# Memory keys by row pieces over four banks, token transposes inside the value projection, first convolution tap on ScalarE

## The chip, the core and the metric

One core of one Trainium2 chip runs the whole layer. The metric is device time in microseconds (us) of one execution. Engines: TensorE (PE in the profile, its weight loads PEld), VectorE (DVE), ScalarE (ACT), GpSimd (POOL) and SyncE (SP), which issues all transfers.

## What is computed

A decoder layer on 256 tokens of width 1024: LayerNorm, a token mixer with three branches (gated delta rule, short convolution, attention into 256 memory tokens), LayerNorm, 32 routed experts of which each token uses four, LayerNorm. The change touches what stands at the start of the mixer:

```python
h = layer_norm(x, ln0_g, ln0_b)
proj = x @ w_in                       # qkv, a, bt, z, xc, gb, gc, qm, gl
qkv = silu(causal_depthwise_conv(qkv, conv_qkv))      # width 4
g = -(exp(a_log) * softplus(a + dt_bias)); beta = sigmoid(bt)
kv = mem @ w_mem_kv; km, vm = split(kv, 2)
```

## The kernel before

All projections of the mixer are made in three products, high part times high part, high times low, low times high, so that single-precision passes suffice. A weight column block of 512 (a "slot", 2 MB) is loaded into one of three raw buffers. It is used in four pieces of 1024 columns per partition. For each piece ScalarE casts the high part (`w_hi`, L1048), and VectorE or GpSimd subtracts it for the low part (`w_lo`, L759); `LO_ENGINE` says which of the two. There are three pairs of piece buffers, so the cast of piece q+3 waits until TensorE has finished with piece q.

One list, `SCHEDULE`, made by `mixer_schedule`, sets the order on every engine: TensorE, ScalarE, VectorE and GpSimd each walk through it and do their part of each entry, so an entry that waits holds back all that follows it on its engine. A "unit" is an entry with a PSUM bank; units take banks 0 to 2 in turn, and one can't start until the bank of the unit three before it is free. Banks 3 to 7 serve the delta rule later.

The start goes like this. SyncE loads the first key columns, the memory tokens (1 MB), three more key column pieces (each 128 columns, rows of 512 bytes), the value columns (2 MB), the tokens `hx` (1 MB), LayerNorm's two parameter rows, small rows, and then the qkv slots. TensorE warms up with ten products (L1222), turns the memory tokens (`memT`, four units, L1244), makes the keys (`km`, four units, one head each, each over all eight row blocks: L1171 to L1173), then the values (`vm`, two units, 128x512 outputs, four row pieces), then turns the normalised tokens (`hT`, four units, L1258), then makes the twelve qkv units of 24 products each (a group of eight "triples"). Between the second and the third stand the eight decay columns (`ab`), then their turn (`abT`).

VectorE does LayerNorm in `ln`: statistics (L1506, L1509), reciprocal, two passes over a tile (L1521, L1523), with ScalarE's root (L1020) in between. Each qkv unit gets four taps on VectorE, a product with a column scalar (L1632) and three multiply-adds (L1635), and the silu on ScalarE (L1027). The decay columns are split on VectorE (`ab split`, L1565, L1566), and their softplus is built from VectorE's min and max (L1655 to L1657) and ScalarE's functions (L1068 to L1071). GpSimd makes all masks at the start (L944 to L965), the per-level ones behind its eighth piece.

After the mixer each expert takes six chunks of 2 MB through a ring of twelve (`chunk_dma`, L792). The second expert's chunks wait until the mixer's last output product is there.

## Time and profile before

| | |
|---|---|
| median of 3 runs | 1269.95 us (1269.81 to 1270.58) |
| profiled execution | 1270.24 us, span 1268.5 us |
| mean granted TensorE clock | 0.987 |
| PE busy | 1218.5 us, 96% |
| DVE, ACT, POOL busy | 400.8, 239.2, 141.1 us (32%, 19%, 11%) |
| DMA | 453.45 MB, 357 GB/s over the span |
| chain that ended last | PE 78%, DMA 9%, SPq 4%, DVE 4% |

The mixer fills the first 340 us or so, the experts the rest. A row of the timeline gives start, duration, engine, line, operation and, in brackets, the idle time before it and what ended that; a group of the lines view gives busy time and mean duration; a window gives the busy time of each engine, the granted clock (PEclk, 1.00 is 2.4 GHz and 0.50 is 1.2 GHz) and the transfers. Matmuls are pipelined, so printed durations overlap, and the spacing of starts tells the pace.

### The profile page before, as it was taken

How to read it: one execution, taken by the hardware profiler on the slowest of the kernel's cores; microseconds unless marked ns; L12 is line 12 of the kernel's file. 1: busy time of each engine (PE TensorE's matmuls, PEld its weight loads, DVE VectorE, ACT ScalarE, POOL GpSimd, SP SyncE). 2: the span in 40 equal slices, each digit the busy share in tenths (PEclk: the TensorE clock that was granted, in tenths of full speed). 3: DMA queues.
4: the chain of work that ended last, by engine and by line, in shares of the span. 5: the costliest groups of instructions: out<-in, count | busy, mean ns of one | idle time of the engine just before them, and what ended most of it. 6: DMA issues, size and time to landing. Idle time of an engine off the chain costs nothing.

```text
span 1268.5 us, 17229 instructions
## 1 busy us (share of the span) xinstructions
PE 1218.5 (96%) x7155; PEld 616.8 (49%) x7155; DVE 400.8 (32%) x787; ACT 239.2 (19%) x385; POOL 141.1 (11%) x105
## 2 busy tenths in 40 slices
PE   8799999999999999999999999999999999999995
PEld 7699999998843333333333333333333333333332
DVE  5685563534521221222222122122122222222114
ACT  4364344444310000010000000000000000000001
POOL 4433422455200000000000000000000000000000
PEclk9899999999999999999999999999999999999998
DMA  9533313595799999999999999999999999999995
GB/s 306 198 134 134 134 68 134 205 360 184 281 399 424 428 427 428 427 428 428 430 428 430 428 427 428 430 428 430 428 427 427 429 427 429 429 426 428 428 427 209
DMA packets 56412, 453.45 MB, mean 357 GB/s; under 512 B 6877, under 2 KB 11050, under 8 KB 31786
## 3 DMA queue, kind: packets, MB, share of 16 engines
q1 hardware_dynamic: 56362, 452.71, 86.3%
q8 instruction: 40, 0.66, 0.2%
q14 instruction: 10, 0.08, 0.0%
HBM read 451.64 MB, written 1.05 MB: 357 GB/s over the span
## 4 chain that ended last, share of the span: by engine, by line
PE 78%; DMA 9%; SPq 4%; DVE 4%; ACT 2%; issue 2%; POOL 0%; another core or an unknown queue 0%; DVEq 0%; ACTq 0%
PE bank L1357 30%; PE bank L1429 15%; DMA late<-in_w_gate_up_dram 8%; PE bank L1171 5%; PE bank L1172 5%; PE bank L1173 5%; PE bank L1328 4%; PE bank L1442 4%; SPq L792 4%; PE bank L1343 2%; PE bank L1417 2%; ACT late L1143 1%; DMA early<-in_ln_b_dram 1%; PE bank L1437 1%; DVE w_lo L759 1%
## 5 line engine op out<-in xcount | busy, mean ns | idle before, releaser
L1357 PE MATMUL bank<-late 128*64 128x512 f32 x1536 | 343.2, 595 | 5.1 <-DMA late<-in_w_gate_up_dram 5.1
L1429 PE MATMUL bank<-late 128*64 128x512 f32 x1024 | 230.1, 602 | 6.2 <-ACT late L1143 6.2
L1357 PEld LDWEIGHTS bank<-late 128*64 128x64 f32 x1536 | 106.7, 137 | 222.7 <-issue 209.8
L1429 PEld LDWEIGHTS bank<-late 128*64 128x64 f32 x1024 | 71.4, 138 | 142.9 <-issue 129.1
L1171 PE MATMUL bank<-act_hi,w_hi 128*128 128x256 f32 x448 | 129.4, 289 | 3.1 <-DVE early L1635 2.5
L1172 PE MATMUL bank<-act_lo,w_hi 128*128 128x256 f32 x448 | 125.8, 281 | 0.0
L1173 PE MATMUL bank<-act_hi,w_lo 128*128 128x256 f32 x448 | 125.8, 281 | 0.0
L1775 DVE TENSOR_SCALAR late<-bank 128x512 f32<-128x512 f32 x32 | 22.1, 692 | 308.2 <-PE bank L1357 308.2
L1357 PE MATMUL bank<-raw,late 128*64 128x512 f32 x512 | 116.7, 598 | 1.2 <-DMA raw<-in_w_gate_up_dram 1.2
L759 POOL TENSOR_TENSOR w_lo<-raw,w_hi 128x1024 fp32r<-128x1024 f32 x33 | 81.2, 2463 | 127.1 <-ACT w_hi L1048 127.1
L1171 PEld LDWEIGHTS bank<-act_hi,w_hi 128*128 128x128 f32 x448 | 84.3, 188 | 5.3 <-DVE early L1635 3.3
L1172 PEld LDWEIGHTS bank<-act_lo,w_hi 128*128 128x128 f32 x448 | 84.5, 189 | 0.1
L1173 PEld LDWEIGHTS bank<-act_hi,w_lo 128*128 128x128 f32 x448 | 84.4, 188 | 0.0
L1786 DVE COPY late<-bank 64x512 f32<-64x512 f32 x32 | 22.2, 694 | 191.3 <-PE bank L1429 191.3
L1136 ACT COPY late<-bank 128x512 f32<-128x512 f32 x33 | 19.3, 586 | 321.9 <-PE bank L1328 321.9
L1048 ACT CAST w_hi<-raw 128x1024 fp32r<-128x1024 f32 x56 | 58.5, 1046 | 90.2 <-issue 59.4
L1357 PEld LDWEIGHTS bank<-raw,late 128*64 128x64 f32 x512 | 34.0, 136 | 72.3 <-issue 69.0
L1442 PE MATMUL bank<-late 64*128 64x512 f32 x256 | 63.6, 615 | 1.0 <-DVE late L1846 1.0
L1145 ACT COPY late<-bank 64x512 f32<-64x512 f32 x32 | 18.5, 579 | 233.3 <-PE bank L1429 233.3
L1328 PE MATMUL bank<-hx,late 128*64 128x512 f32 x264 | 62.3, 592 | 0.0
L1141 ACT ACTIVATE late<-late 128x512 f32<-128x512 f32 x32 | 20.1, 629 | 179.7 <-DVE late L1775 179.7
L1790 DVE COPY late<-bank 128x256 f32<-128x256 f32 x31 | 13.2, 425 | 117.9 <-PE bank L1437 117.9
(319 smaller groups left out, 1194.4 us busy)
## 6 DMA issues: line engine op xcount, KB each, us to landing
late<-in_w_gate_up_dram SPq DMA_DIRECT2D x96, 2048.0 KB, 36.4
late<-in_w_down_dram SPq DMA_DIRECT2D x64, 2048.0 KB, 35.8
raw<-in_w_gate_up_dram SPq DMA_DIRECT2D x32, 2048.0 KB, 34.5
raw<-in_w_in_dram SPq DMA_DIRECT2D x8, 2048.0 KB, 8.7
...
```

What stands on the lines that cost most here:

```text
L759: ops.tensor_tensor(lo, src, as_f32(hi), ALU.subtract).then_inc(split_lo[who], 1)
L792: sp.dma_start(dst, src).then_inc(landed, 16)
L1048: a.copy(hi, src).then_inc(split_hi, 1)
L1171: mm(o, l_hi, r_hi, start=start, stop=False)
L1172: mm(o, l_hi, r_lo, start=False, stop=False)
L1173: return mm(o, l_lo, r_hi, start=False, stop=stop)
L1328: ins = mm(ps[0][64 * c:64 * c + 64, :], onehot[:, t, :], hx[:, t, 512 * c:512 * (c + 1)], start=(t == 0), stop=(t == NT - 1))
L1343: mm(ps[1 + n][64 * c:64 * c + 64, :], e_row[rows, :], bgu[rows, :], start=True, stop=False)
L1357: ins = mm(bk[64 * c:64 * c + 64, :], x_slotT[:, k % 4, 64 * (k // 4):64 * (k // 4) + 64], w[:, kk, at + 512 * c:at + 512 * (c + 1)], star ...
L1417: ins = tr(ps[3][:, c * P:(c + 1) * P], h_tok[:, c:4 * P:4], ident[:])
L1429: ins = mm(ps[3][64 * c:64 * c + 64, :], hidT[:, kk, 64 * q:64 * q + 64], w[:, kk, c * 512:(c + 1) * 512], start=(q == 0 and kk == 0), sto ...
L1442: ins = mm(ps[4 + 2 * t + c][:, :], scatter[64 * c:64 * c + 64, t * P:(t + 1) * P], y_tok[64 * c:64 * c + 64, :], start=False, stop=True, ...
```

## The change

- **Loads.** The memory tokens come first, then key pieces 0 and 1, the tokens, key pieces 2 and 3, LayerNorm's rows, then the value columns in four pieces. All eight key and value pieces are row pieces (256 rows of 512 columns, rows of 2 KB), each with a semaphore. The router's weights move behind slot 5.
- **Keys.** The four heads are made together in banks 4 to 7: for each row piece, 2 row blocks for each of four heads; ScalarE copies all four at the end. Statistics and roots of both tiles come ahead of the keys, the passes in between.
- **Tokens.** The transposes go to banks 4 to 7 too and stand inside the value projection, tile 0 behind its second row piece, tile 1 behind the first tile's third.
- **Who subtracts.** Pieces 0 to 11: DVE, POOL, DVE, POOL, three DVE, two POOL, DVE, POOL, DVE.
- **ScalarE** takes the first tap of each qkv unit (a copy with a column scale), the cast of the decay columns, and the signs and relu of the softplus.
- **GpSimd** makes four of seven block masks first, three behind piece 1, the decay masks behind piece 3, the level masks one by one behind pieces 10 to 20, the chunk masks behind 22.

```diff
@@ -103,10 +103,12 @@
 
 
 
-    order = [("prep", 0)] + [("memT", n) for n in range(4)] + [("prep", 1), ("prep", 2)]
-    order += [("km", n) for n in range(4)] + [("ln", 0, t) for t in range(NT)] + [("vm", n) for n in range(NT)]
-    order += [("hT", t, j) for j in range(2) for t in range(NT)] + [("prep", 9), ("cols",), ("prep", 10)]
-    order += [("qkv", 0), ("ab split",), ("qkv", 1), ("ab", 0), ("qkv", 2), ("abT", 0), ("qkv", 3), ("decay functions",)]
+    order = [("memT", 0), ("prep", 0), ("memT", 1), ("prep", 1), ("memT", 2), ("memT", 3)]
+    order += [("ln stats", t) for t in range(NT)] + [("prep", 2), ("prep", 3)] + [("ln root", t) for t in range(NT)]
+    order += [("km", 0), ("ln", 0, 0), ("prep", 4), ("prep", 5), ("ln", 0, 1), ("prep", 6), ("km copy",), ("prep", 7), ("prep", 8)]
+    order += [("hT", t, j) for t in range(NT) for j in range(2)] + [("prep", 9), ("vm", 0), ("prep", 10), ("vm", 1), ("cols",)]
+    order += [("ab split",)]
+    order += [("qkv", 0), ("qkv", 1), ("ab", 0), ("qkv", 2), ("abT", 0), ("qkv", 3), ("decay functions",)]
...
@@ -392,6 +398,10 @@
 
 
         piece_end, joint = {}, 0
+        for q in PIECES_OF["km", 0]:
+            joint += 1
+            piece_end[q] = (joint_piece, joint) if joint < 4 else (km_full, H)
+        joint = 3
...
@@ -404,7 +414,7 @@
 
 
         LO_ENGINE = ["pool" if q % 2 == 0 or MIXER_SLOTS[q // 4][0] == "br" else "dve" for q in range(4 * N_MIX)]
-        LO_ENGINE[0:12] = ["dve"] * 5 + ["pool"] * 4 + ["dve"] * 3
...
@@ -770,10 +781,14 @@
                 src = m.rearrange("(k p) n -> p k n", p=P)[:, :, c:c + W]
             if n >= RAW:
                 raw_spent(sp, n - RAW)
-            if n == 0:
-                sp.dma_start(dst[:, :, j * P:(j + 1) * P], src[:, :, j * P:(j + 1) * P]).then_inc(piece_in[j], 16)
+            if kind == "kv":
+                sp.dma_start(dst[:, 2 * j:2 * j + 2, :], src[:, 2 * j:2 * j + 2, :]).then_inc(piece_in[4 * n + j], 16)
             else:
                 sp.dma_start(dst, src).then_inc(raw_in[n % RAW], 16)
+
...
@@ -827,14 +842,16 @@
             def bcast(dst, src, done):
                 sp.dma_start(dst, src).then_inc(done, 16)
 
+            sp.dma_start(mem_tok, mem[0].rearrange("(t p) d -> p t d", p=P)).then_inc(mem_in, 16)
             slot_dma(sp, 0, 0)
-            sp.dma_start(mem_tok, mem[0].rearrange("(t p) d -> p t d", p=P)).then_inc(mem_in, 16)
-            for j in range(1, 4):
-                slot_dma(sp, 0, j)
-            slot_dma(sp, 1)
+            slot_dma(sp, 0, 1)
             sp.dma_start(hx[:], x[0].rearrange("(t p) d -> p t d", p=P)).then_inc(x_in, 16)
+            slot_dma(sp, 0, 2)
+            slot_dma(sp, 0, 3)
             bcast(lnp0[:, 0, :], ln0_g.rearrange("(a d) -> a d", a=1).broadcast_to([P, D]), lnp_in[0])
             bcast(lnp0[:, 1, :], ln0_b.rearrange("(a d) -> a d", a=1).broadcast_to([P, D]), lnp_in[0])
+            for j in range(4):
+                slot_dma(sp, 1, j)
...
@@ -1030,16 +1051,16 @@
             a.activation(ln_std[:, 0:1], eps_ln, ACT.Sqrt)
             for s in SCHEDULE:
                 kind = s[0]
-                if kind in ("memT", "hT", "km", "vm", "z", "xc", "gb", "qm", "gate", "pT", "ym", "x1T"):
+                if kind in ("memT", "vm", "z", "xc", "gb", "qm", "gate", "pT", "ym", "x1T"):
                     act.wait_ge(bank_full[bank_of(s)], turn_of(s))
                 free = bank_free[bank_of(s)] if kind not in NOT_UNITS else None
                 if kind == "prep":
                     q = s[1]
                     n = q // 4
-                    if n == 0:
+                    if n < 2:
                         act.wait_ge(piece_in[q], 16)
                     else:
-                        act.wait_ge(raw_in[n % RAW], 16 * len(range(n % RAW or RAW, n + 1, RAW)))
+                        act.wait_ge(raw_in[n % RAW], 16 * len(range(first_fill(n % RAW), n + 1, RAW)))
                     if q >= SPLITS:
                         act.wait_ge(*piece_end[q - SPLITS])
...
@@ -1050,25 +1071,42 @@
                     a.copy(src_hi[:, 2 * s[1]:2 * s[1] + 2, :], bank(s, 512).rearrange("p (a b) -> p a b", a=2)).then_inc(bank_hi, 1)
                 elif kind == "hT":
                     t, j = s[1:]
+                    act.wait_ge(h_turned, 2 * t + j + 1)
                     a.copy(act_hi[:, 4 * j:4 * j + 4, t * P:(t + 1) * P],
-                           bank(s, 512).rearrange("p (a b) -> p a b", b=P)).then_inc(bank_hi, 1)
-                elif kind == "ln":
+                           ps[4 + 2 * t + j][:, :].rearrange("p (a b) -> p a b", b=P)).then_inc(bank_hi, 1)
+                elif kind == "ln root":
+                    ln_root_of(0, s[1])
+                elif kind == "ln" and s[1] == 1:
                     ln_root_of(*s[1:])
-                elif kind == "km":
-                    a.copy(kmT[:, s[1], :], bank(s)).then_inc(free, 1)
+                elif kind == "km copy":
+                    for n in range(H):
+                        act.wait_ge(km_full, n + 1)
+                        a.copy(kmT[:, n, :], ps[4 + n][:, 0:T]).then_inc(km_copied, 1)
+                elif kind == "ab split":
+                    act.wait_ge(ab_in, 16)
+                    a.copy(w_ab_hi[:], w_ab).then_inc(ab_hi, 1)
                 elif kind == "vm":
                     a.copy(vm[:, s[1], :], bank(s, 512)).then_inc(free, 1)
                 elif kind == "qkv":
+                    if s[1] == 0:
+                        act.wait_ge(cols_ready, 1)
+                    act.wait_ge(bank_full[bank_of(s)], turn_of(s))
+                    a.activation(qkvT[:, s[1], :], bank(s), ACT.Copy,
+                                 scale=small_cols[:, 36 + s[1]:37 + s[1]]).then_inc(first_tap, 1)
                     if s[1] >= 1:
                         silu(s[1] - 1)
                     if s[1] == 11:
                         silu(11)
                 elif kind == "decay functions":
-                    act.wait_ge(ab_dve, 1)
-                    a.activation(ea, adt[:, 0, :], ACT.Exp)
-                    a.activation(beta, beta, ACT.Exp, scale=-1.0)
-                    step(a.activation(t_b, t_b, ACT.Exp))
-                    a.activation(t_b, t_b, ACT.Ln, bias=1.0).then_inc(ab_act, 2)
+                    act.wait_ge(bank_free[bank_of(("abT", 0))], turn_of(("abT", 0)))
+                    a.activation(t_c, pre_g, ACT.Relu)
+                    step(a.activation(t_b, pre_g, ACT.Abs))
+                    step(a.activation(ea, adt[:, 0, :], ACT.Exp))
+                    a.mul(ea, ea, -1.0)
+                    step(a.activation(beta, beta, ACT.Exp, scale=-1.0))
+                    a.activation(beta, beta, ACT.Identity, bias=1.0)
+                    step(a.activation(t_b, t_b, ACT.Exp, scale=-1.0))
+                    a.activation(t_b, t_b, ACT.Ln, bias=1.0).then_inc(ab_act, 1)
                 elif kind == "z":
...
@@ -1176,13 +1214,35 @@
 
                 hi, lo = piece(PIECES_OF[s][-1])
                 for k in range(nk):
-                    if s == ("km", 0) and k % 2 == 0:
-                        wait_copied(pe, "memT", k // 2 + 1)
                     if s == ("qkv", 0) and k % 4 == 0:
-                        wait_copied(pe, "hT", 2 + k // 2)
+                        pe.wait_ge(h_split, 3 + k // 4)
                     ins = three(ps[bank_of(s)][:, 0:T], hi[:, k, c * P:(c + 1) * P], lo[:, k, c * P:(c + 1) * P],
                                 rhs_hi[:, k, :], rhs_lo[:, k, :], k == 0, k == nk - 1)
                 ins.then_inc(bank_full[bank_of(s)], 1)
+
+            def project_keys():
+
+                for j in range(4):
+                    hi, lo = piece(PIECES_OF["km", 0][j])
+                    wait_copied(pe, "memT", j + 1)
+                    for n in range(H):
+                        for kk in range(2):
+                            k = 2 * j + kk
+                            ins = three(ps[4 + n][:, 0:T], hi[:, kk, n * P:(n + 1) * P], lo[:, kk, n * P:(n + 1) * P],
+                                        src_hi[:, k, :], src_lo[:, k, :], k == 0, k == KD - 1)
+                        if j == 3:
+                            ins.then_inc(km_full, 1)
+                    if j < 3:
+                        ins.then_inc(joint_piece, 1)
+
+            def turn_tile(t):
+
+                pe.wait_ge(ln_done, t + 1)
+                pe.wait_ge(km_copied, H)
+                for j in range(2):
+                    for k in range(4):
+                        ins = tr(ps[4 + 2 * t + j][:, k * P:(k + 1) * P], hx[:, t, (4 * j + k) * P:(4 * j + k + 1) * P], ident[:])
+                    ins.then_inc(h_turned, 1)
 
             def project_rows(s, lhs_hi, lhs_lo, sums=False, apart=False):
...
@@ -1194,6 +1254,8 @@
                 if apart:
                     order = order[:4] + [(j, t) for t in range(NT) for j in (2, 3)]
                 for j, t in order:
+                    if s == ("vm", 0) and j == 2:
+                        turn_tile(t)
                     u = both[t]
                     hi, lo = piece(PIECES_OF[s][j])
...
@@ -1547,23 +1609,25 @@
                 if kind == "prep":
                     prep_lo(v, d, s[1], "dve")
                     continue
+                if kind == "ln stats":
+                    t = s[1]
+                    if t == 0:
+                        v.wait_ge(x_in, 16)
+                    step(half_stats(t, 0))
+                    step(half_stats(t, 1))
+                    variance(t)
+                    continue
                 if kind == "ln":
                     n, t = s[1:]
                     if n == 0:
-                        if t == 0:
-                            v.wait_ge(x_in, 16)
-                        step(half_stats(t, 0))
-                        step(half_stats(t, 1))
-                        variance(t)
                         v.wait_ge(lnp_in[0], 32)
                         normalise(0, t, lnp0)
                     else:
                         normalise(1, t)
                     continue
                 if kind == "ab split":
```

How it moves the instructions, at three places. ScalarE at the start (`raw` to `w_hi` is a piece's cast, `bank` to `src_hi` a memory block, `bank` to `early` a key head's copy). Before:

```order
L1048 CAST w_hi<-raw 128x1024 [waits piece_in0]
L1050 CAST src_hi<-bank0 128x512 [waits bank_full0]
L1050 CAST src_hi<-bank1 128x512 [waits bank_full1]
L1050 CAST src_hi<-bank2 128x512 [waits bank_full2]
L1050 CAST src_hi<-bank0 128x512 [waits bank_full0]
L1048 CAST w_hi<-raw 128x1024 [waits piece_in1]
L1048 CAST w_hi<-raw 128x1024 [waits piece_in2]
L1048 CAST w_hi<-raw 128x1024 [waits split_lo_dve,bank_full1,piece_in3]
L1058 COPY early<-bank1 128x256 [waits bank_full1]
L1048 CAST w_hi<-raw 128x1024 [waits split_lo_dve,bank_full2,raw_in1]
L1058 COPY early<-bank2 128x256 [waits bank_full2]
```

In the change:

```order
L1071 CAST src_hi<-bank0 128x512 [waits bank_full0]
L1069 CAST w_hi<-raw 128x1024 [waits piece_in0]
L1071 CAST src_hi<-bank1 128x512 [waits bank_full1]
L1069 CAST w_hi<-raw 128x1024 [waits piece_in1]
L1071 CAST src_hi<-bank2 128x512 [waits bank_full2]
L1071 CAST src_hi<-bank0 128x512 [waits bank_full0]
L1069 CAST w_hi<-raw 128x1024 [waits piece_in2]
L1069 CAST w_hi<-raw 128x1024 [waits split_lo_dve,joint_piece,piece_in3]
L1041 ACTIVATE tiny<-tiny 128x1 [waits ln_var] x2
L1069 CAST w_hi<-raw 128x1024 [waits split_lo_pool,joint_piece,piece_in4]
```

The casts of pieces 0 and 1 stand between the memory blocks, and the wait for a bank of a key unit has become one for a piece (`joint_piece`).

TensorE where the tokens are turned (`hx`; L1258 before, L1244 now). Before, at the end of the values:

```order
L1173 MATMUL bank0<-w_hi,src_lo 128x512
L1258 MATMUL bank1<-ident,hx 128x128 [waits ln_done,bank_free1]
L1258 MATMUL bank1<-ident,hx 128x128 x3
L1258 MATMUL bank2<-ident,hx 128x128 [waits ln_done,bank_free2]
L1258 MATMUL bank2<-ident,hx 128x128 x3
L1258 MATMUL bank0<-ident,hx 128x128 [waits ln_done,bank_free0]
L1258 MATMUL bank0<-ident,hx 128x128 x3
```

In the change, inside them:

```order
L1211 MATMUL bank2<-w_hi,src_lo 128x512
L1244 MATMUL bank4<-ident,hx 128x128 [waits km_copied,ln_done]
L1244 MATMUL bank4<-ident,hx 128x128 x3
L1244 MATMUL bank5<-ident,hx 128x128 x4
L1209 MATMUL bank1<-w_hi,src_hi 128x512 [waits split_lo_dve]
```

The transposes wait for the key copies and the tile, no longer for the units' banks, and value products follow them at once.

VectorE between the memory blocks and LayerNorm's passes. Before:

```order
L1626 TENSOR_TENSOR src_lo<-bank0,src_hi 128x512 [waits bank_hi]
L759 TENSOR_TENSOR w_lo<-raw,w_hi 128x1024 [waits split_hi] x4
L1506 BN_STATS tiny<-hx 128x6 [waits x_in]
L1506 BN_STATS tiny<-hx 128x6 [waits dve_chain]
L1509 BN_AGGR tiny<-tiny 128x2 [waits dve_chain]
L1516 RECIPROCAL tiny<-tiny 128x1 [waits ln_root,lnp0_in]
L1521 SCALAR_TENSOR_TENSOR hx<-hx,tiny,early 128x1024 [waits ln_var,dve_chain]
L1523 SCALAR_TENSOR_TENSOR hx<-hx,tiny,early 128x1024 [waits dve_chain]
```

In the change:

```order
L1691 TENSOR_TENSOR src_lo<-bank0,src_hi 128x512 [waits bank_hi]
L1568 BN_STATS tiny<-hx 128x6 [waits x_in]
L1568 BN_STATS tiny<-hx 128x6 [waits dve_chain]
L1571 BN_AGGR tiny<-tiny 128x2 [waits dve_chain]
L1568 BN_STATS tiny<-hx 128x6
L1568 BN_STATS tiny<-hx 128x6 [waits dve_chain]
L1571 BN_AGGR tiny<-tiny 128x2 [waits dve_chain]
L770 TENSOR_TENSOR w_lo<-raw,w_hi 128x1024 [waits split_hi]
L1578 RECIPROCAL tiny<-tiny 128x1 [waits ln_root,lnp0_in]
L1583 SCALAR_TENSOR_TENSOR hx<-hx,tiny,early 128x1024 [waits ln_var,dve_chain]
```

The low part of the third piece (the one L770 row) stands behind both tiles' statistics.

## Rows read from the trace of the kernel before

**Rows 1.** Page, part 2: GB/s of all DMA in each of the 40 slices
```profile
GB/s 306 198 134 134 134 68 134 205 360 184 281 399 424 428 427 428 427 428 428 430 428 430 428 427 428 430 428 430 428 427 427 429 427 429 429 426 428 428 427 209
```

**Rows 2.** Chain that ended last, 1040 to 1268.5: start us, us, what
```profile
1181.68 48.84 DMA late<-in_w_gate_up_dram
```

**Rows 3.** Windows of 5 us: PE, PEld, DVE, ACT, POOL busy, PEclk, DMA, GB/s
```profile
330.00:335.00 5.00, 5.00 (x23) 4.01 (x22) 1.79 (x3) 0.38 (x1) 2.34 (x7) 1.00 0.72 262
```

**Rows 4.** Timeline, SyncE, 334 to 345: start us, us, queue line op
```profile
336.37 1.28 SPq L792 DMA_DIRECT2D late<-in_w_gate_up_dram  x3
```

**Rows 5.** Timeline, TensorE: start us, us, operation [idle before, what ended it]
```profile
7.44 3.42 PE L1244 MATMUL bank<-ident,early 128*128 128x128 f32 x16 [2.14 <-DMA early<-in_mem_dram]
...
34.48 0.50 PE L1171 MATMUL bank<-w_hi,src_hi 128*128 128x512 f32 x1 [3.48 <-POOL w_lo L759]
...
51.91 0.28 PE L1171 MATMUL bank<-act_hi,w_ab_hi 128*8 128x256 f32 x1 [4.14 <-DVE w_ab_lo L1566]
...
63.63 0.38 PE L1171 MATMUL bank<-act_hi,w_hi 128*128 128x256 f32 x1 [1.13 <-DVE early L1635]
...
95.26 0.39 PE L1171 MATMUL bank<-act_hi,w_hi 128*128 128x256 f32 x1 [1.41 <-DVE early L1635]
```

**Rows 6.** Windows of 2 us, TensorE alone: busy, PEclk, DMA share, GB/s
```profile
8.00:10.00 2.00, 2.00 (x11) 0.50 1.20 291
...
52.00:54.00 2.00, 2.00 (x11) 0.53 1.05 396
...
62.00:64.00 2.00, 0.87 (x8) 1.00 0.00 0
```

**Rows 7.** Groups by line, TensorE, 12:22, 23:30, 35:39, 336:342: xcount, busy us, mean ns
```profile
L1173 PE MATMUL bank<-src_hi,w_lo 128*128 128x256 f32 x29 | 8.2, 281 | 0.0
...
L1171 PE MATMUL bank<-w_hi,src_hi 128*128 128x512 f32 x10 | 4.0, 395 | 0.0
...
L1173 PE MATMUL bank<-w_hi,src_lo 128*128 128x512 f32 x4 | 2.3, 569 | 0.0
...
L1258 PE MATMUL bank<-ident,hx 128*128 128x128 f32 x16 | 2.1, 274 | 0.4 <-DVE hx L1519 0.4
```

**Rows 8.** Windows of 2 us, all engines, value columns in rows of 2 KB
```profile
14.00:16.00 2.00, 2.00 (x18) 2.00 (x18) 1.74 (x2) 1.32 (x2) 0.00 (x0) 1.00 1.06 390
```

**Rows 9.** Timeline, ScalarE: casts, a bank copy, a table load, short function, silu
```profile
11.38 2.00 ACT L1048 CAST w_hi<-raw 128x1024 fp32r<-128x1024 f32 x2
...
14.96 0.36 ACT L1058 COPY early<-bank 128x256 f32<-128x256 f32 x1
...
64.05 1.28 ACT L1068 ACT_TABLE_LOAD   x1
...
66.47 0.19 ACT L1069 ACTIVATE tiny<-tiny 128x8 f32<-128x8 f32 x1
...
70.59 0.42 ACT L1027 ACTIVATE early<-early 128x256 f32<-128x256 f32 x1
```

**Rows 10.** Timeline, VectorE: low parts, statistics, tile passes, decay cast, taps
```profile
12.46 2.36 DVE L759 TENSOR_TENSOR w_lo<-raw,w_hi 128x1024 fp32r<-128x1024 f32 x2 [0.26 <-ACT w_hi L1048]
...
21.95 1.42 DVE L1506 BATCH_NORM_STATS2 tiny<-hx 128x6 f32<-128x512 f32 x2 [1.43 <-DMA hx<-in_x_dram]
...
24.86 2.43 DVE L1521 SCALAR_TENSOR_TENSOR hx<-hx,tiny,early 128x1024 f32<-128x1024 f32 x1
...
27.33 1.28 DVE L1523 SCALAR_TENSOR_TENSOR hx<-hx,tiny,early 128x1024 f32<-128x1024 f32 x1
...
49.28 2.15 DVE L1565 CAST w_ab_hi<-early 128x64 fp32r<-128x64 f32 x1
...
61.55 0.48 DVE L1632 TENSOR_SCALAR early<-bank,small_cols 128x256 f32<-128x256 f32 x1
...
62.06 1.52 DVE L1635 SCALAR_TENSOR_TENSOR early<-bank,small_cols,early 128x255 f32<-128x255 f32 x3
```

**Rows 11.** Timeline, GpSimd: low part beside VectorE's pass
```profile
23.81 2.40 POOL L759 TENSOR_TENSOR w_lo<-raw,w_hi 128x1024 fp32r<-128x1024 f32 x1 [0.38 <-ACT w_hi L1048]
```

114 lines of the change are left out of this document (60 added, 54 removed).

## The prediction

> **What bounds the kernel now.** Read the page by slices first, then the chain that ended last, the DMA windows, and only then the start. The 40 slices (31.7 us each) show 424 to 430 GB/s from the thirteenth to the last but one, and a stream with gaps before [rows 1]. The chain agrees at its end: the last link before the last expert's products is a weight chunk, 48.84 us from issue to landing [rows 2], so the expert stage ends when its weights have come. The windows tell since when the stream is unbroken: the engines still idle a quarter of the time at 330 to 335 us [rows 3]. SyncE issues three chunks of the second expert from 336.37 [rows 4], when the last output product of the mixer is there. What follows is a fixed amount of bytes at a fixed rate, about 932 us to the end of the span (1268.5). The expert stage, 73% of the span, is thus a rigid block behind the mixer's last product, and TensorE's work in it hangs on the same point. A microsecond taken out of TensorE's path in the mixer is one off the total; a faster expert stage isn't in this change.
>
> In the mixer TensorE is the path, and its holes stand at the start: 2.14 us before the memory tokens are turned, 3.48 before the last value product, 4.14 before the decay columns, 1.13 before the fifth qkv unit, then 1.41 at 95 us [rows 5]. Three of them also cost clock: the granted clock is 0.50 behind the first (1.2 of 2.4 GHz) and 0.53 behind the third; it stays at 1.00 around the hole of 1.13 [rows 6]. Behind the second hole a 128x512 product takes 569 ns, against 395 at full clock [rows 7].
>
> **The ledger.** I count TensorE's time up to the fifth qkv unit, which starts at 63.63 now [rows 5]. All its products stay; only order and waits change. At full clock 29 triples fit in 10 us at width 256 (0.35 each), 10 in 7 us at width 512 (0.70), and 16 transposes take 2.1 us [rows 7].
>
> *Landing.* The memory tokens go first. Now they land at 7.44 behind a half-megabyte column piece; without it, 0.52 MB at between 291 and 390 GB/s, 1.3 to 1.8 us earlier: 5.9. Row pieces then come in 2 KB rows. The window with column pieces (512 B rows) gave 291 GB/s, one with whole rows 390 [rows 8]. At 390 a piece (0.52 MB) takes 1.3 us and the tokens (1.05 MB) 2.7: piece 0 at 7.2, piece 1 at 8.6, tokens at 11.3, pieces 2 and 3 at 12.7 and 14.0, LayerNorm's rows near 17, value pieces from 18. At 291 all of it would be later by a third, 3 us at piece 3; this end is kept for the range.
>
> *Keys.* ScalarE's cast is 1.0 us in a row of casts [rows 9], VectorE's subtraction 1.2, GpSimd's 2.4 [rows 10, 11]. Piece 0: cast 7.3 to 8.3, low part to 9.6, so the keys start at 9.6 (10.55 now). 32 triples are 11.2 us. Piece 1 goes to GpSimd and is ready at 12.4, as the first 2.8 us end. Piece 2 goes to VectorE but stands behind both tiles' statistics. Two halves take 1.42 and the aggregate 0.2; four memory subtractions end at about 12.0, so the statistics end at 15.2, and the low part at 16.4, where the products of piece 1 end at 15.3: a wait of **1.0**.
>
> *Values and token transposes.* 16 triples of 0.70 are 11.2; the 16 transposes inside them 2.1 at full clock. Their inputs: low parts of value pieces 0 and 1 at 22, normalised tiles at 20.6 and 25.9 (two passes of 1.28 [rows 10] behind LayerNorm's rows and the interleaved low parts), key copies at 24.9, all before TensorE wants them (22, 25, 28, 31 us). The 3.48 hole goes: piece 3 of the values is cast behind the first value piece, not behind the second tile's root. If that cover were gone, up to 3.5 us would come back.
>
> *Decay columns.* The 4.14 hole consists of three taps, the cast of the columns (2.15 [rows 10], the span in which GpSimd runs a subtraction) and their subtraction, all on VectorE behind the first unit. Now ScalarE casts (0.2) and VectorE subtracts ahead of the first taps, under 11 us of products. The hole and its slow clock go. Small turn 0.2, five groups of 8 triples 14.0, turn of the decay rows 0.2.
>
> *First tap.* VectorE loses 12 operations of 0.48 [rows 10], ScalarE gains 12. The trace has no scaled copy of 128x256 from a bank: below it the plain copy, 0.36, above it the silu, 0.42 [rows 9]; I take 0.42, since it reads a scale. It runs beside the low part, so of the bank's return, cast 1.05, low part 1.25, three taps 1.52 [rows 10], it adds nothing on odd pieces and the bank comes back 0.5 earlier. The hole of 1.13 behind the short decay unit becomes 0.9.
>
> *Decay signs.* ScalarE now does eight short functions (0.2 each, chained; four before) and two table loads of 1.28 in one go [rows 9], about 4.1 us. This holds back the cast for the eighth unit: about 0.45 us of wait. The hole of 1.41 shrinks by 0.5. These two cancel.
>
> *Masks.* Four levels end by 7.7 and three run between subtractions; per-level masks, 0.8 us each, fill GpSimd behind even pieces, in a stretch where it has one 2.4 us subtraction per two units (5.7 us). They cost nothing unless VectorE's subtraction meets one (0.5). Router weights move four loads later and are needed 290 us later: nothing. SyncE reaches all it is moved past earlier than now.
>
> *Hand-offs and clock at the start.* 0.8 for some ten new waits near the edge, 0.5 for slow clock around 8 us (0 if the warm-up carries over, 1.8 if it is as behind the 3.48 hole [rows 5, 7]: some 12 products at 0.38 instead of 0.23 apart).
>
> Sum: 9.6 + 11.2 + 1.0 + 11.2 + 2.1 + 0.2 + 14.0 + 0.2 + 0.9 + 0.8 + 0.5 = 51.7, or 52.2 with the rounding of triples (0.354). 63.63 − 52.2 = **11.4 us**. The profiled execution took 1270.24 (span 1268.5); that less 11.4 is **1258.8**. The median shown is 0.3 lower, which is noise here.
>
> **Where it is tight.** The low part of piece 2 (VectorE, ready to start at 15.2) and of piece 3 (GpSimd, ready at 14.0 + 1.05 = 15.1 to 15.6) reach their engines within half a microsecond. The trace shows what a meeting costs: the pass over a tile that starts at 24.86 takes 2.43, its twin 1.28 [rows 10], while GpSimd's 2.40 from 23.81 runs [rows 11]: it did nothing until GpSimd was done. [...]
>
> **Rivals.**
> 1. *GpSimd gets in first.* Piece 2's low part ends at 18.7, the wait is 3.3 instead of 1.0, and a hole of 3.48 was followed by the half clock (1.8 us). Plus 4.1: **1262.9**. For it: tokens landed late in this trace (21.95 [rows 10], though issued at 8.96). Against it: pieces land late too, which holds GpSimd back.
> 2. *Better than the ledger.* Rows land at full rate, neither the 1.0, the 0.8 nor the 0.5 shows and the taps' hole closes: 3.2 less, **1255.6**.
> 3. *The gain is hidden.* If the stream were bound by something of its own, nothing would move: **1270.2**. Against it: the windows before 335 us, in which DMA idles [rows 3], and the issue that waits for the mixer [rows 4].
> 4. *Slower: a split before each piece.* The keys now stop at each quarter. If each split starts only when the piece before it is being used and the two engines lock each other out, a hole of 3.3 and a slow restart of 1.8 stand before each of four pieces: 4 x 5.1 − 1.0 = 19.4 more, **1278**. It decides from the third such piece on (14.3 > 11.4). For it: one product group per piece is 2.8 us, less than cast plus GpSimd's 2.4. Against it: three buffers, and pieces alternate engines. The Trainium skill, TensorE: Matmul & The Clock Gate, section HAM oscillation — how this bites in real kernels, describes this pattern, a wait behind each short group that drops the clock again each time; this trace shows such drops behind the holes of 2.14, 3.48 and 4.14 and none at 1.13 [rows 5 to 7]; no run here shows them in a row.
>
> **How the numbers follow.** Forecast 0.47, rival one 0.33, two 0.13, three 0.03, four 0.04. The range runs from just above rival two, 1255.8, to above rival one with a little of slow landing, 1264. A difference of 0.2% (2.5 us) is what can be told from no change. Faster needs under 1267.4: forecast and the first two rivals, 0.93. Same 0.03, slower 0.04.
>
> **What would show it.** Right: memory transposes start near 6 and keys at 9.5; one hole of about 1 us before the third key piece and none over 1 before 50; the decay columns start without a hole; the fifth qkv unit starts at 52, the unbroken stream near 325; clock 1.00 from 12 us on. A subtraction of 2 us or more at 15 with 0.50 clock behind it is rival one. Four holes of 3 us with a clock drop behind each are rival four. Wrong altogether: a mixer that ends 11 us earlier and a span that doesn't.

## The result, and the profile after

| | before | change |
|---|---|---|
| median of the runs made side by side | 1269.88 us (1269.34 to 1270.58, 4) | 1255.13 us (1254.24 to 1257.27, 4) |
| profiled execution, its span | 1270.24, 1268.5 | 1255.70, 1254.0 |
| mean granted clock | 0.987 | 0.994 |
| PE, DVE, ACT, POOL busy | 1218.5, 400.8, 239.2, 141.1 | 1213.0, 390.5, 243.5, 148.7 |
| DMA | 357 GB/s over the span | 362 GB/s |

The ratio is 0.9887, interval 0.9875 to 0.9899: 14.75 us less by the medians. The forecast was 11.4 less, 1258.8, in a range from 1255.8. So the kernel is faster by the expected way, and by 3.4 us more than forecast, 0.7 us beyond the lower end of the range.

Page of the change, parts 2 and 4: bandwidth by slice, then the shares of the chain that ended last.

```profile
GB/s 335 221 148 143 70 136 67 330 292 201 353 409 429 428 429 428 427 429 429 429 428 429 429 429 428 429 428 430 428 429 427 427 427 428 429 427 428 428 427 198
...
PE 78%; DMA 8%; SPq 5%; DVE 3%; ACT 3%; issue 2%; POOL 0%; DVEq 0%; ACTq 0%
```

From the thirteenth slice to the last but one it reads as in [rows 1], 427 to 430 GB/s. The block of expert weights is as rigid as it was; it only begins earlier. Its chunks, in SyncE's part of the timeline (start, duration, line, operation, count), first of the kernel before, then of the change. The row of before is the whole group whose last three chunks [rows 4] show:

```profile
330.44 21.24 SPq L792 DMA_DIRECT2D late<-in_w_gate_up_dram  x5
```

```profile
315.57 21.13 SPq L807 DMA_DIRECT2D late<-in_w_gate_up_dram  x5
```

The group starts 14.9 us earlier. The windows of 5 us around it in the change (columns as in [rows 3]):

```profile
315.00:320.00 5.00, 5.00 (x23) 4.01 (x22) 1.79 (x3) 0.52 (x1) 2.48 (x7) 1.00 0.72 261
320.00:325.00 5.00, 4.57 (x35) 3.99 (x34) 4.03 (x10) 1.81 (x6) 0.00 (x0) 1.00 0.86 321
325.00:330.00 5.00, 4.75 (x43) 4.54 (x43) 3.89 (x17) 2.28 (x6) 0.00 (x0) 1.00 1.01 433
```

The window at 315 (261 GB/s, 23 products) is the image of the one at 330 before [rows 3]: the same work 15 us earlier. The stream is unbroken from 325.

TensorE's timeline in the change (start, duration, line, operation; in brackets the idle time before and what ended it):

```profile
7.89 0.66 PE L1308 MATMUL bank<-ident,early 128*128 128x128 f32 x4 [0.53 <-DVE src_lo L1691]
9.63 0.38 PE L1209 MATMUL bank<-src_hi,w_hi 128*128 128x256 f32 x1 [1.09 <-DVE w_lo L770]
...
15.80 0.39 PE L1209 MATMUL bank<-src_hi,w_hi 128*128 128x256 f32 x1 [0.23 <-DVE w_lo L770]
...
21.71 0.50 PE L1209 MATMUL bank<-w_hi,src_hi 128*128 128x512 f32 x1
...
27.40 1.03 PE L1244 MATMUL bank<-ident,hx 128*128 128x128 f32 x8
...
34.76 0.36 PE L1209 MATMUL bank<-act_hi,w_hi 128*128 128x256 f32 x1
...
40.53 0.28 PE L1209 MATMUL bank<-act_hi,w_ab_hi 128*8 128x256 f32 x1
...
50.14 0.39 PE L1209 MATMUL bank<-act_hi,w_hi 128*128 128x256 f32 x1 [0.63 <-DVE early L1699]
...
81.55 0.39 PE L1209 MATMUL bank<-act_hi,w_hi 128*128 128x256 f32 x1 [0.81 <-DVE early L1699]
```

Against [rows 5]: the holes of 3.48 and 4.14 are gone (the tokens' transposes and the decay columns follow the product before them with none), and the one of 2.14 has become 0.53. The hole before the fifth qkv unit is 0.63 (1.13 before), and the one before the sixteenth unit 0.81 (1.41). The keys start at 9.63, the values at 21.71, the first qkv unit at 34.76, the fifth at 50.14 (63.63 before) and the sixteenth at 81.55 (95.26). The gain is thus 13.5 us at the fifth unit, 13.7 at the sixteenth, 14.5 at the end of the span.

The 13.5 are of two kinds. The holes printed up to the fifth unit add up to 11.5 us before and to 2.5 in the change. The half clock behind three of them, in windows from 7 to 12, 35 to 39 and 52 to 56 us, held back 5.1 us of products before (an estimate: one minus the granted clock, summed over windows of 1 us), and nothing in the change. By that estimate 5.1 of the 13.5 are clock and the rest is waiting. One window of 2 us from the middle stretch of before, TensorE alone:

```profile
36.00:38.00 2.00, 2.00 (x6) 0.50 1.04 395
```

VectorE, then GpSimd, at the third and fourth key piece:

```profile
11.47 1.42 DVE L1568 BATCH_NORM_STATS2 tiny<-hx 128x6 f32<-128x512 f32 x2
...
14.58 1.17 DVE L770 TENSOR_TENSOR w_lo<-raw,w_hi 128x1024 fp32r<-128x1024 f32 x1
...
16.80 2.28 DVE L1583 SCALAR_TENSOR_TENSOR hx<-hx,tiny,early 128x1024 f32<-128x1024 f32 x1
19.11 1.29 DVE L1585 SCALAR_TENSOR_TENSOR hx<-hx,tiny,early 128x1024 f32<-128x1024 f32 x1
```

```profile
9.90 2.42 POOL L770 TENSOR_TENSOR w_lo<-raw,w_hi 128x1024 fp32r<-128x1024 f32 x1 [2.19 <-ACT w_hi L1069]
...
15.09 2.90 POOL L770 TENSOR_TENSOR w_lo<-raw,w_hi 128x1024 fp32r<-128x1024 f32 x1 [0.60 <-ACT w_hi L1069]
```

The meeting that rival one was about did come, but the other way round. VectorE was in 0.5 us before GpSimd, kept its 1.17, and it was GpSimd that took 2.90 in place of 2.42. The later pass over a tile, which starts at 16.80 within GpSimd's 2.90, took 2.28; its twin at 19.11 took 1.29, as in [rows 10].

ScalarE's new work, the first tap and the decay signs with their two table loads:

```profile
50.54 0.47 ACT L1094 ACTIVATE early<-bank,small_cols 128x256 f32<-128x256 f32 x1
...
51.22 0.20 ACT L1102 ACTIVATE tiny<-tiny 128x8 f32<-128x8 f32 x1
...
51.53 1.28 ACT L1104 ACT_TABLE_LOAD   x1
...
53.73 1.28 ACT L1109 ACT_TABLE_LOAD   x1
55.02 0.21 ACT L1109 ACTIVATE tiny<-tiny 128x8 f32<-128x8 f32 x1
```

The tap takes 0.47 (0.42 was assumed), and the signs with all eight functions go from 51.22 to 55.23, 4.0 us (4.1 forecast).

### The profile page after: what moved, and what is told of

Read it like the earlier page. It is cut to its first block, busy times and chain, and to the rows that moved or that the text cites. A ratio compares the mean times of both kernels' runs of the same rounds, so it can differ in the third digit from the quotient of the medians.

```text
span 1254.0 us, 17233 instructions
## 1 busy us (share of the span) xinstructions
PE 1213.0 (97%) x7155; PEld 613.1 (49%) x7155; DVE 390.5 (31%) x768; ACT 243.5 (19%) x402; POOL 148.7 (12%) x106
## 4 chain that ended last, share of the span: by engine, by line
PE 78%; DMA 8%; SPq 5%; DVE 3%; ACT 3%; issue 2%; POOL 0%; DVEq 0%; ACTq 0%
PE bank L1419 29%; PE bank L1491 15%; DMA late<-in_w_gate_up_dram 8%; PE bank L1209 6%; SPq L807 5%; PE bank L1210 5%; PE bank L1211 5%; PE bank L1504 4%; PE bank L1390 4%; PE bank L1405 2%; PE bank L1479 1%; ACT late L1181 1%; ACT w_hi L1069 1%; PE bank L1499 1%; DMA raw<-in_w_mem_kv_dram 0%
## 5 line engine op out<-in xcount | busy, mean ns | idle before, releaser
L770 POOL TENSOR_TENSOR w_lo<-raw,w_hi 128x1024 fp32r<-128x1024 f32 x33 | 81.9, 2483 | 102.1 <-ACT w_hi L1069 102.0
## 6 DMA issues: line engine op xcount, KB each, us to landing
raw<-in_w_mem_kv_dram SPq DMA_DIRECT2D x8, 512.0 KB, 11.2
```

The lines of the kernel that those rows point to most:

```text
L770: ops.tensor_tensor(lo, src, as_f32(hi), ALU.subtract).then_inc(split_lo[who], 1)
```

## The experiments

In each the change is the base unless another is named. A median is of the number of runs in brackets. The mark used throughout is where the sixteenth unit starts, 81.55 in the first profile of the change and 81.82 in the second, so a difference of 0.3 there is nothing. "Later" is counted from 81.55.

**The memory second** (`mem_second`): the old order of the first two loads.

```diff
-            sp.dma_start(mem_tok, ...).then_inc(mem_in, 16)
             slot_dma(sp, 0, 0)
+            sp.dma_start(mem_tok, ...).then_inc(mem_in, 16)
```

> The change, but the first key piece is loaded ahead of the memory tokens, as before. Theory A (the gain is holes and slow clock ahead of the fifth qkv unit): the tokens land 1.3 us later, at 7.2 instead of 5.9, the memory transposes start behind a hole of 1.3 to 2 and partly at the slow clock, the keys start at 10.3 to 11 instead of 9.6, and the total rises by 0.7 to 2.5 us. Rival B (the load order of the first megabytes doesn't matter, because value pieces and LayerNorm's rows set the pace later): 0 within 0.3 us.

1257.64 us (4). The memory blocks start at 7.42 and the keys at 10.95, and the sixteenth unit at 82.94, 1.4 later. The memory tokens have the longer way to the first key product (transposes, copies, subtractions), and the half megabyte in front of them holds them back by 1.6 us (5.83 in the change).

**Decay columns split late** (`split_late`): the split where it was, both halves on VectorE.

```diff
-    order += [("ab split",)]
-    order += [("qkv", 0), ("qkv", 1),
+    order += [("qkv", 0), ("ab split",), ("qkv", 1),
@@
...
-                    a.copy(w_ab_hi[:], w_ab).then_inc(ab_hi, 1)
@@
...
+                    step(d.tensor_copy(w_ab_hi[:], w_ab))
```

> The change, but the decay columns are split on VectorE behind the first qkv unit's taps, as before. Theory A: a hole of 1.4 to 3.5 us stands again before the decay columns and, from about 2 us on, a stretch at the slow clock behind it; the total rises by 1.5 to 5 us. Rival B (the hole came from VectorE's first tap and GpSimd's subtraction, both gone now): under 0.7 us.

1257.96 us (4), the sixteenth unit at 83.70, 2.15 later.

```profile
42.61 0.28 PE L1205 MATMUL bank<-act_hi,w_ab_hi 128*8 128x256 f32 x1 [1.61 <-DVE w_ab_lo L1627]
```

VectorE there:

```profile
42.01 0.19 DVE L1626 CAST w_ab_hi<-early 128x64 fp32r<-128x64 f32 x1
42.23 0.23 DVE L1627 TENSOR_TENSOR w_ab_lo<-early,w_ab_hi 128x64 fp32r<-128x64 f32 x1
```

Of the 4.14 hole of before, 1.61 comes back. The other 2.5 are the cast, 0.19 against 2.15 [rows 10], with no subtraction of GpSimd across it any more (before, one ran from 49.04 to 51.38), and the first tap of 0.48, now on ScalarE. So about half of this hole was a meeting of the two engines, and here it is gone although the split stands where it stood. The clock stays at 1.00 behind 1.61.

**Tokens turned behind the values** (`turn_behind`):

```diff
-                    if s == ("vm", 0) and j == 2:
-                        turn_tile(t)
@@
                         project_rows(s, src_hi, src_lo)
+                        turn_tile(0)
+                        turn_tile(1)
```

> The change, but both tiles are transposed behind the value projection instead of inside it. Theory A: the casts of four blocks and their subtractions are no longer covered, so the first qkv unit waits about 1.2 us, the second up to 1 more for its piece; total up by 1 to 2.5 us. Rival B (the place of the transposes is worth nothing, only the order of the casts removed the 3.48 us hole): 0 within 0.4 us.

1256.41 us (4), the sixteenth unit at 83.30, 1.75 later.

```profile
36.46 0.36 PE L1209 MATMUL bank<-act_hi,w_hi 128*128 128x256 f32 x1 [1.31 <-DVE act_lo L1673]
```

The transposes themselves cost about the same at either place (1.91 in one row of 16 here, two rows of 1.03 in the change); what the place inside the values hides is the copy and the subtraction behind them, 1.31.

**First tap on VectorE** (`tap_vector`):

```diff
...
-                    a.activation(qkvT[:, s[1], :], bank(s), ACT.Copy,
-                                 scale=small_cols[:, 36 + s[1]:37 + s[1]]).then_inc(first_tap, 1)
@@
-                    v.wait_ge(first_tap, c + 1)
+                    full()
+                    step(d.tensor_scalar(o, bk[:, 0:T], small_cols[:, 36 + c:37 + c], None, ALU.mult))
```

> The change, but the first tap of the twelve qkv units is on VectorE as before. Theory A: the holes of 0.63 before the fifth unit and 0.81 behind the decay exponentials grow to about 1.1 and 1.4, total up by 0.9 to 1.3 us. Rival B (VectorE's load in the qkv stage was a bound of its own, and 12 operations of 0.48 come back in full): up by 3 to 5.8 us.

1256.13 us (4), the sixteenth unit at 82.06, 0.5 later. Its hole is back to what [rows 5] show before (1.44, and 1.14 before the fifth unit):

```profile
82.06 0.39 PE L1204 MATMUL bank<-act_hi,w_hi 128*128 128x256 f32 x1 [1.44 <-DVE early L1695]
```

Twelve operations of 0.48 moved off VectorE, 5.8 us of its busy time, are worth 0.5 us at the mark (1.0 by the medians): only the two holes moved.

**Signs on VectorE** (`signs_vector`): min, max and the sign product on VectorE, four functions on ScalarE.

```diff
-                    a.activation(t_c, pre_g, ACT.Relu)
-                    step(a.activation(t_b, pre_g, ACT.Abs))
...
+                    step(d.tensor_scalar(t_a, pre_g, -1.0, None, ALU.mult))
+                    d.tensor_tensor(t_b, t_a, pre_g, ALU.min).then_inc(ab_dve, 1)
+                    step(d.tensor_scalar(t_c, pre_g, 0.0, None, ALU.max))
```

> The change, but the decay signs, relu and doubling by one are on VectorE again. Theory A: small operations of VectorE meet GpSimd's subtraction (one of them took 2.04 us before), no hole on TensorE grows by more than 0.5 us, and the fifth unit starts where it does in the change, 50.1; total 0 to +1 us. Rival B (these operations set the decay path): 2 us or more.

One run: 1254.86, the sixteenth unit at 82.24, 0.4 to 0.7 later, with a hole of 0.68 before the delta rule's first small products (0.25 in the change). By the total this edit isn't told from nothing.

**Masks as before** (`masks_whole`): seven block masks and the decay masks first, level and chunk masks behind piece 8.

```diff
-            block_masks(range(0, 4))
-            LEVEL_AFTER = {10: 0, 12: 1, 14: 2, 16: 3, 18: 4, 20: 5}
+            block_masks(range(0, LEVELS + 1))
+            decay_masks()
...
```

> The change, but all block and decay masks are made at the start and all level and chunk masks in one go behind the eighth piece. Theory A: GpSimd is busy with masks until about 12 us instead of 7.7, so the second key piece is subtracted from about 12.2 instead of 9.9 and its products start 1.5 to 2.5 us late; the level masks (about 7 us from 28.5 on) hold back the pieces of the third and fifth... units by less than their slack; total up by 1.5 to 4 us. Rival B (the masks are hidden either way): 0 within 0.4 us.

One run: 1256.92, the sixteenth unit at 83.17, 1.6 later. TensorE, then GpSimd:

```profile
15.06 0.39 PE L1205 MATMUL bank<-src_hi,w_hi 128*128 128x256 f32 x1 [2.24 <-POOL w_lo L770]
```

```profile
12.65 5.70 POOL L770 TENSOR_TENSOR w_lo<-raw,w_hi 128x1024 fp32r<-128x1024 f32 x2
```

GpSimd comes to the second key piece at 12.65 instead of 9.90, and TensorE has a hole of 2.24 for it. Making part of the masks later is thus a condition of the earlier keys, not a gain beside them.

**The meeting forced** (`meeting`): VectorE's third key piece waits until GpSimd has ended the fourth, which is rival one made to happen.

```diff
+                    if s[1] == 2:
+                        v.wait_ge(split_lo["pool"], 2)
                     prep_lo(v, d, s[1], "dve")
```

> The change, but VectorE's subtraction of the third key piece is made to wait for GpSimd's of the fourth, which is the prediction's first rival made to happen. Theory A (a hole of 3 us there also costs clock): the third piece is ready at 19.2 instead of 15.75, a hole of 3.5 to 4 us, a granted clock of 0.5 behind it, total up by 4.5 to 6 us. Rival B (later waits, for value pieces that land from 18 us on, absorb part): up by 2 to 3.5 us.

1260.31 us (4), ratio to before 0.992 (0.9904 to 0.9937). The sixteenth unit starts at 85.88, 4.3 later. TensorE; then its windows of 2 us (busy, granted clock, DMA share, GB/s); then VectorE:

```profile
18.80 0.39 PE L1209 MATMUL bank<-src_hi,w_hi 128*128 128x256 f32 x1 [3.19 <-DVE w_lo L770]
```

```profile
16.00:18.00 2.00, 0.00 (x0) 1.00 1.05 402
18.00:20.00 2.00, 1.20 (x7) 0.82 1.05 389
20.00:22.00 2.00, 2.00 (x12) 0.50 1.06 382
22.00:24.00 2.00, 2.00 (x16) 0.83 1.08 392
```

```profile
17.52 1.23 DVE L770 TENSOR_TENSOR w_lo<-raw,w_hi 128x1024 fp32r<-128x1024 f32 x1 [2.82 <-POOL w_lo L770]
```

Rival one was priced at 4.1 us and is worth 4.3 at the mark (4.5 to 5.2 by the medians): a hole of 3.19 in place of 0.23, and the half clock (1.2 GHz), which TensorE fell to behind it. The price was right and the case didn't come.

**Tokens last** (`tokens_late`): the tokens' load behind the value pieces, the rest as in the change.

```diff
-            sp.dma_start(hx[:], ...).then_inc(x_in, 16)
@@
                 slot_dma(sp, 1, j)
+            sp.dma_start(hx[:], ...).then_inc(x_in, 16)
```

> The change, but the tokens are loaded behind all eight key and value pieces. Theory A: pieces 2 and 3 land 2.7 us earlier, but VectorE stands at the statistics until the tokens land at about 21, with piece 2 behind them; the third key piece is then ready at about 25, a hole of 9 us; total up by 8 to 11 us. Rival B (the tokens have slack): under 1 us.

One run: 1267.61, the sixteenth unit at 93.74, 12.2 later, more than was expected. TensorE, then VectorE:

```profile
26.25 0.58 PE L1209 MATMUL bank<-src_hi,w_hi 128*128 128x256 f32 x1 [10.49 <-DVE w_lo L770]
```

```profile
21.92 1.42 DVE L1568 BATCH_NORM_STATS2 tiny<-hx 128x6 f32<-128x512 f32 x2 [10.17 <-DMA hx<-in_x_dram]
```

The statistics stand before the third key piece on VectorE. A load that the keys don't need then holds them for 10.49 us, and nearly the whole gain is gone. The granted clock is at or near 0.50 from 21 to 31 us; what of this lies behind the hole costs time too, and the expectation of 8 to 11 had left it out.

**Value columns in one load** (`values_whole`): one 2 MB transfer of 512-column rows, all four pieces waiting for its end.

```diff
+            if n == 1:
+                if j == 0:
+                    sp.dma_start(dst, src).then_inc(piece_in[4], 16)
...
@@
-                        act.wait_ge(piece_in[q], 16)
+                        act.wait_ge(piece_in[min(q, 4)], 16)
```

> The change, but the value columns come as one transfer of 2 MB. Theory A: they land at 22 to 23 instead of from 17.9 on, the first value piece is split at 25.3 instead of 21.6, and a hole of about 3.5 us with a slow clock behind it stands before the values; sixteenth unit at 85 to 87.5. Rival B (the two passes over a tile on VectorE set the pace there): under 1 us.

One run: 1263.19, the sixteenth unit at 87.05, 5.5 later.

```profile
25.64 0.51 PE L1212 MATMUL bank<-w_hi,src_hi 128*128 128x512 f32 x1 [3.77 <-DVE w_lo L770]
```

Bytes and their order are the same; only the moment at which the first quarter may be used is later, and a half clock at 26 to 30 us follows the hole.

**The change's loads in the kernel before** (`early_loads_b`): only the order of the transfers. The key pieces stay column pieces and the values one transfer.

```diff
+            sp.dma_start(mem_tok, ...).then_inc(mem_in, 16)
             slot_dma(sp, 0, 0)
-            sp.dma_start(mem_tok, ...).then_inc(mem_in, 16)
-            for j in range(1, 4):
-                slot_dma(sp, 0, j)
-            slot_dma(sp, 1)
+            slot_dma(sp, 0, 1)
             sp.dma_start(hx[:], ...).then_inc(x_in, 16)
+            for j in range(2, 4):
+                slot_dma(sp, 0, j)
...
+            slot_dma(sp, 1)
```

> The kernel before with the change's order of loads alone (first key piece with the memory and its keys' loads as the change has them), the rest of the start as before. Theory A, the gain sits in work that the new order of loads must be joined with (value turns inside the projection, tap and signs on ScalarE, masks in parts): the time is 0 to 4 us below before's, the keys start near 9.5 us, the norm's parts lie at 17 to 20 us, and the hole of 4.14 us at 51.91 stays. Theory B, the order of loads carries nearly all: 8 to 12 us below before.

1274.92 us (5), before on the same chip 1270.52, ratio 1.0038 (1.0024 to 1.0052): **slower**, by 4.4 us. Neither theory had that sign. TensorE, then ScalarE:

```profile
6.09 1.53 PE L1245 MATMUL bank<-ident,early 128*128 128x128 f32 x12 [0.69 <-DMA early<-in_mem_dram]
10.81 0.66 PE L1245 MATMUL bank<-ident,early 128*128 128x128 f32 x4 [3.19 <-DVE src_lo L1627]
...
27.38 0.50 PE L1172 MATMUL bank<-w_hi,src_hi 128*128 128x512 f32 x1 [2.85 <-DVE w_lo L759]
...
40.11 0.50 PE L1172 MATMUL bank<-w_hi,src_hi 128*128 128x512 f32 x1 [2.54 <-POOL w_lo L759]
```

```profile
7.85 1.04 ACT L1049 CAST w_hi<-raw 128x1024 fp32r<-128x1024 f32 x1 [5.57 <-DMA raw<-in_w_mem_kv_dram]
8.80 1.55 ACT L1051 CAST src_hi<-bank 128x512 fp32r<-128x512 f32 x3
...
25.02 1.04 ACT L1049 CAST w_hi<-raw 128x1024 fp32r<-128x1024 f32 x1 [7.60 <-DMA raw<-in_w_mem_kv_dram]
```

The memory tokens are there at 6.09, as planned. But ScalarE's list has the cast of piece 0 ahead of the memory blocks, so they wait until 8.80 with a full bank each, and TensorE stands 3.19 for the fourth. The value columns, still one load and now behind the tokens, can be cast only at 25.02, which opens a hole of 2.85. The one before the last value product, 3.48 in [rows 5], stays as 2.54, and the one of 4.14 stays whole. The fifth unit starts at 67.60, 4.0 later than before. So this order of loads has no worth of its own. In the same way, what the edits cost when they are undone one by one (1.4, 2.2, 1.8, 0.5, 0.5, 1.6 above, 8 us in all) isn't the list of what each would bring alone. The keys over four banks weren't tried alone.

**Idle products before the output projection** (`warm_change`): aimed at the hole of 2.16 us in the mixer.

```diff
                 elif kind == "wo":
+                    if s[1:] == (0, 0):
+                        keep_warm(8, ps[7])
```

> The change, with eight idle products of TensorE (1 us of the hole of 2.16 us at 297 us) before the output projection. Theory A: the runs of the change that differ by 3 us among themselves (1254.2 to 1257.3) differ by whether the granted clock falls behind this hole; filled, the clock stays, and the runs lie at 1254 to 1254.5, none above 1255.5. Rival B (the spread has another cause): median 1255.1 and the same spread, or up to 1 us more, if the products delay the real ones.

1259.68 us (4; 1257.52 to 1260.80). A miss of aim: the products stand at the output projection, 2.4 us behind the start of the work that the hole held up. The hole stayed (2.14 at 297.47), and the products run in the half clock behind it:

```profile
299.91 2.60 PE L1284 MATMUL bank<-ident 128*128 128x128 f32 x16
```

It says only that idle products in the wrong place cost: the unit marks up to 81.59 are those of the change, and the median is about 4 us above. Some 2 of the 4 are the products themselves (the table further down has it); where the rest lies isn't shown, since the profiled execution is the fastest of the four.

**Idle products in the hole** (`warm_hole`), with the **change again** (`change_again`) beside it, five rounds each.

```diff
+                if s == ("br", 0, KD - 1):
+                    keep_warm(8, ps[7])
```

> The change itself, unaltered, on the chip of the next three. It fixes the spread. Theory A: its runs lie between 1254 and 1258, and the total of one run goes with the number of slow-clock stretches in the mixer behind 290 us (each 1.5 us). In the profile the sixteenth unit starts at 81.5 to 81.7 whatever the total. Rival B: the start itself varies, by a microsecond or more.

> The change with eight idle products in the hole of 2.16 us that stands before the last branch unit (at 295 to 297 us in the change), the place that warm_change missed. Theory A: 1.9 of the 2.16 us are filled, no slow stretch follows at 298 to 304, and the median lies 0.5 to 1.7 us under that of the change on the same chip. Rival B: the granted clock falls all the same (here or a few us later), as in warm_change, and the median is equal or up to 3 us higher.

The change again: 1255.84 us (5; 1254.12 to 1259.77), ratio 0.989. With the hole filled: 1255.55 (5; 1254.09 to 1255.86), ratio 0.9879 (0.9862 to 0.9895). The medians differ by 0.3, which is nothing; the highest of five by 3.9, which five runs don't settle. What the second profile of the change does show is the behaviour of the clock. Windows of 2 us, TensorE alone, first of it (behind a hole of 2.16), then of `mem_second` (2.15):

```profile
300.00:302.00 2.00, 2.00 (x10) 1.00 0.04 8
```

```profile
300.00:302.00 2.00, 2.00 (x9) 0.50 0.00 0
```

The same work behind the same wait runs at 2.4 GHz in one execution and at 1.2 in the other.

**Idle products in the hole of the kernel before** (`warm_before_b`): the same two lines.

> The kernel before with eight idle products put into the hole of 2.15 us at 310.73 in the mixer. Theory A, the rest of the change's gain beyond its earlier start is fewer stretches at the half clock behind 290 us: no slow stretch at 310 to 316 us, and the time is 0.7 to 1.7 us below before's. Theory B, those stretches have no part in it: within 0.4 us of before.

1268.55 us (10), before beside it 1270.52 (14), ratio 0.9988 (0.9978 to 0.9998): 2.0 less by the medians, 0.3 to 2.8 by the interval, which holds A's 0.7 to 1.7 and is clear of B only in part. Run by run: five of ten lie at 1267.18 to 1267.90, with a granted clock of 0.992 to 0.994; none of the fourteen of before is under 1268.87 or over 0.991. Its profile is one of the slower ones (1270.14). Windows of 5 us:

```profile
310.00:315.00 5.00, 4.62 (x30) 3.98 (x29) 3.69 (x10) 2.06 (x4) 1.03 (x1) 1.00 0.42 177
...
340.00:345.00 5.00, 4.85 (x33) 4.88 (x34) 3.11 (x15) 2.67 (x7) 0.00 (x0) 0.76 1.01 429
345.00:350.00 5.00, 5.00 (x28) 4.92 (x28) 2.75 (x15) 0.71 (x5) 0.00 (x0) 0.55 1.02 436
```

The stretch at 310 runs at 1.00 (0.66 in the same window before). In windows of 2 us the slow clock lies at 342 to 350 instead, twice as long as the stretch at 344 to 350 before, and again at 376 to 380: this execution lost as much as the profiled one of before, only elsewhere. The five faster executions left no trace, so where their clock stayed up isn't shown.

## Why the prediction was right, and where it failed

**What bounds the kernel: right.** What the change moves on TensorE lies before 41 us, what it moves elsewhere ends with the last masks at 89. The gain is 13.7 at the sixteenth unit and 14.5 at the end, and all sixteen profiles keep that: from the sixteenth unit to the end of the span they take 1170.5 to 1174.4 us, wherever that unit starts between 81.6 and 99.2.

**The ledger, term by term**, up to the fifth unit:

| term | forecast | profile of the change |
|---|---|---|
| keys start | 9.6 | 9.63 |
| keys with the wait in them | 11.2 + 1.0 | 12.08 (to 21.71) |
| values and token transposes | 11.2 + 2.1 | 13.05 (to 34.76) |
| five groups, two turns, last hole | 0.2 + 14.0 + 0.2 + 0.9 | 15.38 (to 50.14) |
| hand-offs, slow clock, rounding | 0.8 + 0.5 + 0.5 | none beyond the rows above |
| fifth unit | 52.2 | 50.14 |

The four lines of work came within 0.3 us each. **The step that failed is "Hand-offs and clock at the start"**, 0.8 for ten new waits and 0.5 for slow clock. No such time shows up: the printed holes between 9.63 and 50.14 are 0.23 and 0.63, and the windows of 2 us from 6 to 52 show a clock of 1.00 throughout. The first two, around the holes of 0.53 and 1.09:

```profile
6.00:8.00 2.00, 1.47 (x13) 1.24 (x13) 0.69 (x1) 1.31 (x2) 1.51 (x4) 1.00 1.08 409
8.00:10.00 2.00, 0.91 (x7) 0.67 (x8) 1.65 (x2) 2.00 (x4) 0.10 (x1) 1.00 1.02 412
```

(PE, PEld, DVE, ACT, POOL busy, clock, DMA share, GB/s.) The hole of 2.14 had been followed by the half clock; the holes of 0.53 and 1.09 are not, and [rows 5, 6] pointed that way, since the clock stayed at 1.00 around 1.13. The wait of 1.0 before the third key piece is a hole of 0.23: the statistics started at 11.47 rather than 12.0, and the piece was ready at 15.75 instead of 16.4. The rounding was real (32 times 0.354 is 11.33, not 11.2), but it is already within the four lines above: of the keys' 12.08, 11.33 are products, and the other 0.75 are this hole and the wider spacing of the products around it, where 1.0 had been put. Together the fifth unit starts 2.06 us before the forecast's 52.2.

**Where the 3.4 us beyond the forecast lie.** Of them, 2.1 lie before the fifth unit. From there to the sixteenth unit it is 0.2: the hole of 1.41 shrank to 0.81, and the signs on ScalarE took back less than that, where the prediction let the two cancel. The last microsecond lies behind 290 us, where the ledger had no term. Sorted by the number of stretches at the half clock between 290 and 400 us (each some 3.4 us long, 1.7 us of products lost), the time from the sixteenth unit to the end of the span is:

| stretches | profiles | us |
|---|---|---|
| none | `change_again`, `warm_hole`, `signs_vector` | 1170.5 to 1170.9 |
| one | `mem_second`, `split_late`, `turn_behind`, `meeting`, `masks_whole`, `tokens_late` | 1171.9 to 1172.3 |
| one, products added outside the hole | `warm_change` | 1174.2 |
| two | the change's first profile | 1172.5 |
| three (in `warm_before_b` two of them joined) | before, `early_loads_b`, `warm_before_b`, `tap_vector`, `values_whole` | 1172.9 to 1174.4 |

So an execution of the change in which the clock doesn't fall there gains up to 2.7 us more (1170.5 against 1173.2), and the medians (14.75 against 13.7 at the start) show about 1 of it. Five of ten executions of `warm_before_b` agree by their times and granted clocks. Why the stretches come less often in the change, with the hole of 2.16 unaltered, isn't settled: `values_whole` and `tap_vector` have three as before. Nor are they tied to that hole: the change's first profile has none behind it, but two at 330 to 334 and 360 to 364, the first of them with no printed hole above 0.43 between 298 and 330.

**Rivals.** *One, GpSimd first*: didn't happen, by half a microsecond; `meeting` makes it happen and gives 4.3 for 4.1. The Trainium skill, SBUF — State Buffer, section Who interferes with whom, states that VectorE and GpSimd share a pair of ports, that this pair is an exclusive lock, and that issue order decides who blocks. This trace agrees in both directions: GpSimd's 2.90 against 2.42 when VectorE was first, VectorE's 2.28 against 1.29 when GpSimd was. Such a rule leaves open which engine comes first, and that was the rival's whole condition. *Two, better than the ledger* (1255.6): its total is what came, and in part for its reasons: no hand-offs, no slow clock, a short wait. But the taps' hole didn't close (0.63), so 2.1 of its 3.2 us came where it put them, and the clock behind 290 us, which it doesn't name, made up the rest; that the total fits so closely is in part luck. Its chance of 0.13 was too low, and a range that ends at its edge left no room for anything behind the ledger. *Three, hidden*: no, the stream moved with the mixer. *Four, a split before each piece*: no piece of the keys but the third shows a wait, so it didn't decide; but `early_loads_b` and `masks_whole` show its like, holes of 3.19, 2.85, 2.54 and 2.24 where an engine's list is in the wrong order for the loads. With all the companions left out the kernel is slower than before (`early_loads_b`); with one left out, it stayed 2 us (`tokens_late`) to 15 us (`signs_vector`) faster than before.

**Edits costed at nothing.** The masks in parts: right as costed, and 1.6 if undone. The first tap: 0.5 of hole where 0.2 was written. The decay columns' hole: closed as forecast, and 2.15 if its split stays late.
